# Where the band mask of a windowed attention is added: by TensorE as a product, or by VectorE with the row maximum

## The reference

```
s = einsum(q, k) * 64 ** -0.5                      # 128 queries x up to 384 keys
s = where((|i - j| <= 128) & inside, s, -1e30)
m = maximum(max(s), sink)
p = where(mask, exp(s - m), 0)
probs = p / (sum(p) + exp(sink - m))
o = probs @ v
```

## Time and profile before

| | |
|---|---|
| time, median of 3 runs | 2214.48 us (2213.93 to 2215.01) |
| the profiled execution's own time | 2217.88 us |
| its span, first to last instruction | 2216.1 us |
| mean granted TensorE clock | 0.994 |
| TensorE busy | 2167.8 us, 98% |
| VectorE, ScalarE, GpSimd busy | 1461.8, 825.3, 337.5 us |
| softmax attention, first to last score product | about 942 to 1143 us |

### The profile page before, as it was taken

How to read it: one execution, slowest core, us unless ns; L and a number is a source line. 1 busy time by engine, 2 the same in 40 slices (tenths; PEclk the granted TensorE clock), 3 DMA queues, 4 the chain that set the end, 5 groups by cost and what they waited for, 6 DMA issues and landing times.

```text
span 2216.1 us, 32719 instructions
## 1 busy us (share of the span) xinstructions
PE 2167.8 (98%) x12054; PEld 1917.9 (87%) x12054; DVE 1461.8 (66%) x2571; ACT 825.3 (37%) x1676; POOL 337.5 (15%) x327
## 2 busy tenths in 40 slices
PE   6999999999999999999999999899999999999998
PEld 5999999999888888877778788899999999988887
DVE  7666676667665776866653456767676766657676
ACT  7233222222343345644443333422222232333343
POOL 6111111111100002110002244311211111100000
PEclk8999999999999999999999999999999999999999
DMA  3322222232676555432255873132223222387554
GB/s 125 99 80 80 93 92 92 93 109 81 230 259 204 182 186 160 139 96 78 72 146 166 268 222 110 47 99 86 92 93 110 80 80 92 109 291 252 171 189 163
DMA packets 245746, 300.19 MB, mean 135 GB/s; under 512 B 24146, under 2 KB 159698, under 8 KB 245588
## 3 DMA queue, kind: packets, MB, share of 16 engines
q1 hardware_dynamic: 236948, 284.98, 40.2%
q10 hardware_dynamic: 8640, 13.11, 1.7%
HBM read 206.29 MB, written 88.47 MB: 133 GB/s over the span
## 4 chain that ended last, share of the span: by engine, by line
PE 89%; DVE 5%; DMA 2%; issue 2%; ACT 1%; SPq 0%; POOL 0%; DVEq 0%; POOLq 0%; ACTq 0%
PE ps L2291 15%; PE ps L2287 12%; PE ps L2289 9%; PE ps L2290 9%; PE ps L2299 7%; PE ps L2301 7%; PE ps L2300 7%; PE ps L2213 4%; PE ps L2215 4%; PE ps L2214 4%; PE ps L2480 1%; PE ps L2491 1%; PE ps L2231 1%; PE ps L2233 1%; PE ps L2232 1%
## 5 line engine op out<-in xcount | busy, mean ns | idle before, releaser
L2291 PE MATMUL ps<-hs,w_lo 128*128 128x384 f32 (+1 forms) x992 | 305.4, 308 | 0.0
L2299 PE MATMUL ps<-w_hi,dh 128*128 128x512 f32 x770 | 300.6, 390 | 2.0 <-DVE w_lo L1838 0.8
L2301 PE MATMUL ps<-w_hi,dh 128*128 128x512 f32 x770 | 299.7, 389 | 0.0
L2300 PE MATMUL ps<-w_lo,dh 128*128 128x512 f32 x610 | 237.4, 389 | 0.0
L1835 DVE TENSOR_TENSOR dh<-dr,dh 128x640 fp32r<-128x640 f32 x154 | 127.2, 826 | 165.5 <-ACT dh L1284 165.4
L1245 ACT CAST w_hi<-w_raw 128x512 fp32r<-128x512 f32 x220 | 135.8, 617 | 236.1 <-PE ps L2291 228.7
L2289 PE MATMUL ps<-hs,w_hi 128*128 128x384 f32 (+1 forms) x644 | 215.3, 334 | 6.9 <-DVE hs L1687 4.2
L1284 ACT CAST dh<-dr 128x640 fp32r<-128x640 f32 x154 | 112.0, 727 | 276.0 <-PE ps L2301 254.6
L2290 PE MATMUL ps<-hs,w_hi 128*128 128x384 f32 (+1 forms) x644 | 214.5, 333 | 0.0
L2287 PE MATMUL ps<-hs_first,w_hi 128*128 128x512 f32 x588 | 210.9, 392 | 0.7 <-DVE second_u L1779 0.7
L2287 PE MATMUL ps<-hs,w_hi 128*128 128x512 f32 x588 | 210.2, 391 | 0.0
(11 more groups left out here) (290 smaller groups left out, 4620.9 us busy)
## 6 DMA issues: line engine op xcount, KB each, us to landing
dr<-hid_mid SPq DMA_DIRECT2D x154, 320.0 KB, 3.2
w_raw<-in_w_ffn_down SPq DMA_DIRECT2D x176, 256.0 KB, 3.6
hid_mid<-st SPq DMA_DIRECT2D x88, 320.0 KB, 2.2
w_raw<-in_w_ffn_gate SPq DMA_DIRECT2D x44, 512.0 KB, 5.4
w_raw<-in_w_ffn_up SPq DMA_DIRECT2D x44, 512.0 KB, 5.1
hid_mid<-sg SPq DMA_DIRECT2D x66, 320.0 KB, 2.2
hq<-o_mid SPq DMA_DIRECT2D x70, 128.0 KB, 3.3
w_raw<-in_w_in SPq DMA_DIRECT2D x14, 512.0 KB, 4.9
```

The costliest lines, as they stand in the source:

```text
L2291: last = mm(out, lo[:, k, :], b_hi, start=False, stop=k == 3, skip_group_check=True)
L2299: mm(out, hi, w_h, start=first and p in D_FRESH, stop=False, skip_group_check=True)
L2300: mm(out, hi, w_l, start=False, stop=False, skip_group_check=True)
L2301: return mm(out, lo, w_h, start=False, stop=last, skip_group_check=True)
```

## The change

TensorE no longer adds the mask: the products of lines 2470 to 2477 go, with TensorE's waits for the identity and the window, and the score products start their sums themselves. VectorE's single reduction over both heads becomes two operations, one for each head. Each reads the scores from PSUM and the band from SBUF, writes their sum back over the scores, and folds the sum's maximum, from -1e30 on, into a column of `stats`. The band `band` has three tiles, before (edge), middle (zeros) and behind (edge), so that one operation reads it over the unit's whole width; `first` skips the tile before where a unit has none. `T["negm"]` now counts four steps a unit instead of three. The bf16 identity and its copy in the first FFN are gone; `to_mid` gets shorter and moves.

```
-        ident_bf = sb("ident_bf", [P, P], BF16)
+        to_mid = sb("to_mid", [P, TT])
...
-        wmask = sb("wmask", [P, 2, P], BF16)
+        band = sb("band", [P, 3, P], BF16)
         later = sb("later", [P, P], BF16)
-        to_mid = sb("to_mid", [P, P // 2])
...
-        ONES, IDENT_BF, NEG_SINKS = 1, 2, 3
+        ONES, NEG_SINKS = 1, 2
...
-            act.wait_ge(T["window"], 2)
+            act.wait_ge(T["window"], 3)
...
-                    act.wait_ge(T["negm"], 3 * n + 3)
+                    act.wait_ge(T["negm"], 4 * n + 4)
...
-                        v.tensor_copy(ident_bf[:, :], ident[:, :]).then_inc(const_set, 1)
...
-            v.tensor_copy(wmask[:, :, :], window_f[:, :, :]).then_inc(T["window"], 1)
+            v.memset(band[:, 1, :], 0.0).then_inc(T["window"], 1)
+            v.tensor_copy(band[:, 0:3:2, :], window_f[:, :, :]).then_inc(T["window"], 1)
...
                     dve.wait_ge(T["s"], n + 1)
-                    v.reduce_max(st[:, MX, :], ps[:, 0:2, 0:(hi - lo) * P], AX.X).then_inc(T["negm"], 1)
-                    dve.wait_ge(T["negm"], 3 * n + 1)
+                    if n == 0:
+                        dve.wait_ge(T["window"], 3)
+                    first = 0 if lo < b else 1
+                    for e in range(2):
+                        scored = ps[:, e, 0:(hi - lo) * P]
+                        v.tensor_tensor_reduce(out=scored, in0=scored,
+                                               in1=band[:, first:first + hi - lo, :].rearrange("p m k -> p (m k)"),
+                                               scale=1.0, scalar=NEG, op0=ALU.add, op1=ALU.max,
+                                               accum_out=st[:, MX, e:e + 1]).then_inc(T["negm"], 1)
+                    dve.wait_ge(T["negm"], 4 * n + 2)
...
-            pe.wait_ge(const_set, IDENT_BF)
-            pe.wait_ge(T["window"], 2)
...
                     for e in range(2):
-                        if hi - lo == 3:
-                            edges = ps[:, e, :].rearrange("p (a s q) -> p a s q", a=2, s=2)[:, :, 0, :]
-                            mm(edges, ident_bf[:, :], wmask[:, :, :], start=True, stop=False, skip_group_check=True)
-                        elif lo < b:
-                            mm(ps[:, e, 0:P], ident_bf[:, :], wmask[:, 0, :], start=True, stop=False, skip_group_check=True)
-                        else:
-                            mm(ps[:, e, P:2 * P], ident_bf[:, :], wmask[:, 1, :], start=True, stop=False,
-                               skip_group_check=True)
-                    for e in range(2):
                         half = slice(e * HD, (e + 1) * HD)
                         last = mm(ps[:, e, 0:(hi - lo) * P], q_rot[j % 2][half, b * P:(b + 1) * P],
-                                  kT[half, lo * P:hi * P], start=False, stop=True, skip_group_check=True)
+                                  kT[half, lo * P:hi * P], start=True, stop=True)
```

More of the change, by code:

```diff
@@ L1544, in keep_o @@
                             act.wait_ge(gn["sum"], TT * h + t - 1)
-                        nc.scalar.activation(wmask[:, t % 2, :], ps[:, O_BANKS[c], t * P - c0:(t + 1) * P - c0], ACT.Square,
+                        nc.scalar.activation(band[:, t % 2, :], ps[:, O_BANKS[c], t * P - c0:(t + 1) * P - c0], ACT.Square,
                                              accum_out=grs[:, h % 2, t:t + 1]).then_inc(gn["sum"], 1)
```

## The result

The changed kernel takes 2223.6 us (median of 5 runs, 2221.53 to 2228.66) against 2214.48 (now of 5 runs too, 2212.42 to 2218.30); ratio 1.004, 95% interval 1.0029 to 1.0051. The forecast was 2207.5 us, faster, in a range of 2203.0 to 2213.0: the measured time lies 10.6 us above it. The profiled execution took 2221.93 us with a span of 2220.1, 4.0 us more than the span before.

A forecast was written before the change was run, and what follows sets the result against it. TensorE's instructions were taken to bound the attention stage, busy 214.00 of 214.00 us. 7.0 us leave and nothing comes: 2214.5 - 7.0 = 2207.5 us, range 2203.0 to 2213.0.

The forecast's parts named there:

- What leaves TensorE: Attention stage: dropping the mask products takes 7.0 us off TensorE's queue, 10.6 us at the upper end.
- rival A: Attention stage: the masks' whole hold on TensorE goes, 10.6 us, giving 2203.9 us; chance 0.17.
- What VectorE gets: Attention stage: two operations per unit replace one reduction, lengthening the way from scores to maximum by 0.32 us.
- X: Growth per attention unit of the way from scores to maximum; forecast 0.32 us, lower bound -0.1.
- What hides X: Attention stage: TensorE's slack before next scores and VectorE's waits for scores hide X, so nothing stalls.
- The cover: Time VectorE waits for scores per attention unit, available to hide X after the change; forecast 0.60 us.
- rival C: Attention stage: VectorE's loop becomes the bound from X = 0.60 us on, 2226.5 or 2245 us; chance 0.14.
- After the stage: Behind attention, 1240 to 1280 us: loads are released by TensorE and move with it, so the gain lasts.
- rival B: At 1240 to 1280 us DMA-bound loads make TensorE wait up to 5.3 us longer, 2212.8 us; chance 0.13.
- Edits at nothing: Identity copy, band setup, moved waits and shifted tiles priced at nothing; band setup under 0.4 us if uncovered.
- the slower one: The same as rival C: VectorE's loop bounds the attention stage; chance 0.14.

The follow-up runs named there:

- E1: Changed kernel with 192 unused bytes per partition behind `to_mid`, restoring the old tile addresses; 2207.88 us, ratio 0.9961 to the kernel before.
- E9: E1 with the old reduction over both heads in place of the two new operations, so no mask at all; 2206.84 us, ratio 0.9959.
- E11: E1 with one extra VectorE reduction over both heads' scores in each unit; 2215.95 us, ratio 0.9995.
- E2: Kernel before, masks kept, with `to_mid` and the bf16 identity swapped so tiles between lie 192 bytes lower; 2234.33 us, ratio 1.008.
- E6: Changed kernel with 64 unused bytes ahead of all tiles and 192 behind `to_mid`: new addresses, old distance; 2207.28 us, ratio 0.9961.
- E7: E1 with only the `dh` tiles of the second FFN's down projection 64 bytes higher; 2214.63 us, ratio 0.9994.
- E3: Changed kernel with a gap of 64 bytes ahead of all tiles, weight tiles included; 2225.77 us, ratio 1.0041.
- E5: Changed kernel with 192 unused bytes ahead of all tiles: activations at old addresses, weights moved along; 2226.01 us, ratio 1.0043.
- E4: Changed kernel with 64 unused bytes behind `to_mid`; 2234.11 us, ratio 1.0078.
- E8: Changed kernel with 128 unused bytes behind `to_mid`; 2225.39 us, ratio 1.0046.

## Why the prediction was wrong, point by point

- **What leaves TensorE:** right. 7.0 us forecast, 7.3 measured in the changed kernel, 6.7 in E1. The 0.09 us between full-array and half-array products stayed (0.74 us from transposes to scores, 0.75 forecast), so rival A, 10.6 us, is out. This row agrees with the rule of the Trainium skill, TensorEngine Tiling (Array Packing), section Tiling Modes, that a change of tiling mode drains TensorE.
- **What VectorE gets:** right in kind, too high in size. X = (1062.30 - 1061.12) - (1070.63 - 1069.63) = 0.18 us in a wide unit instead of 0.32. The new operation takes 583 and 448 ns for 384 and 256 elements, (583 - 448)/128 = 1.05 ns an element, as the subtraction does. It does have an instruction of its own for the maximum, 141 ns, but that lies beside the next operation. The half-rate rule that the Trainium skill, Vector Engine (DVE) Microarchitecture Reference, section Points that are easy to get wrong, has for two non-bf16 SBUF sources did not bite here, with one source in PSUM and the other in bf16: 1.05 ns an element is the subtraction's rate.
- **What hides X:** right; E9 shows it. The cover was under-sized, 0.60 us against some 0.87 by the estimate from E11, so the point from which rival C decides was set too low. VectorE's waits for scores fell to 18.7 + 5.3 = 24.0 us, not to 16.
- **After the stage:** right. The loads moved with TensorE, and rival B is out: the wait for the added tile did not grow. It was 5.3 us before, 2.2 in the changed kernel and 2.5 in E1. This is no gain of the change: it was 2.9 us in E2, which still has the masks, and 4.7 in E6, which hasn't, so it differs from kernel to kernel with no order that the runs show. E1 gained 8.5 us (2216.40 - 2207.88) where 7 were forecast; its interval, 0.9949 to 0.9974, holds 7 us too.
- **Edits at nothing:** this is the step that failed. "All tiles behind the smaller ones move together" priced the move at 0, and it cost 6.1 + 7.0 = 13.1 us in the two down projections, and 480 output products by 4.4 ns or 2 us besides. They do move together, but not with the weight tiles ahead of them, and where they lie against the weights is what counted. None of the rivals had it: the slower one had VectorE as its mechanism.

By the sum of the profiles: -7.3 + 13.1 - 1.7 (the piece with the shorter wait) - 0.1 = +4.0 us. The medians differ by 9.1 us; with 7 us gained, that leaves 16 for the layout, against 17.6 from E1 and E2. The down and output products account for 15 of it. E1 is the version that beats both kernels, 0.9961; E6 equals it.

## What to carry to other kernels

A change that adds, drops or resizes a tile moves all tiles behind it, and should be priced for the stages that it doesn't edit. Before the trace of such a change is read for its mechanism, compare the distance between starts of the same products in a stage that was not touched; then repeat the change with its addresses padded back. In this kernel that turned a loss of 0.4% into a gain of 0.4%.

## What the runs showed of the hardware

Two operands of fp32r products (128 x 128 stationary, 512 columns streamed), at a granted clock of 1.00:

| distance of the operands' starts, modulo 256 bytes | kernels | ns between down products | down projections, us | gate and up 1, us |
|---|---|---|---|---|
| 0 | before, E1, E6, E7 (all but the second down), E9 to E11 | 226.7 | 284.7 to 284.9, 265.2 | 507.7 to 509.6 |
| 64 | changed, E2, E3, E5, E7 (second down) | 233.3 | 290.9 to 291.1, 272.2 | 508.4 to 510.8 (without E7) |
| 128 | E4 | 232.5 | 290.1, 271.3 | 514.7 |
| 192 | E8 | 228.3 | 286.7, 267.6 | 512.4 |

The duration of a weight load is the same in both (median 187 ns after, 188 before). In the down and output projections the activation is stationary and the weight streamed; in gate, up and input products it is the other way round, and there 64 costs nothing clear (77.6 us from input to scores in both kernels). By the mean distance of starts in gate and up 1, before and after, it is 116.7 and 119.2 ns for 256 columns, 173.4 and 173.1 for 384, 229.4 and 230.3 for 512: an effect of 1 to 2 us, no more than the stage's own scatter. The distance of a product's own two operands is not the whole of it. In the output projection 120 of the 480 products stream `w_hi3` or `w_lo3`, which lie in the same region as `hq`: their distance is 0 modulo 512 in every kernel. Yet between two such products in a row (80 pairs) the mean distance of starts is 227.7 ns before, but 230.2 in the changed kernel, 232.5 in E4, 232.9 in E8, and 230.4 in E5, where both operands of these products have the very addresses of the kernel before. So something else takes part, their neighbours' operands or the accesses of other engines; no run tells which.

That the cause is the load of a stationary tile beside the streaming of another product's columns, both out of the same memory, is argued, not shown. In the down products distances of 0 modulo 512 were not tried; all fast kernels have 39680, which is 256 modulo 512.
